# Expert outputs of a mixture layer: per-token gathers from DRAM in place of one-hot scatters on the matmul engine

## The reference

```python
logits = (xt @ router_w).astype(jnp.float32)
top_val, top_idx = lax.top_k(logits, TOP_K)            # TOP_K = 2
gates = jax.nn.softmax(top_val, axis=-1)
combine = jnp.einsum("nk,nke->ne", gates, jax.nn.one_hot(top_idx, N_EXPERTS, dtype=jnp.float32))
y = jnp.zeros((B * T, D), dtype=jnp.float32)
for e in range(N_EXPERTS):
    y = y + combine[:, e:e + 1] * swiglu(xt, w_gate[e], w_up[e], w_down[e]).astype(jnp.float32)
```

## Time and profile before

| what | value |
|---|---|
| median of 3 runs | 1693.59 us |
| lowest, highest | 1688.69, 1699.33 us |
| the profiled execution | 1676.64 us |
| its span | 1674.8 us |
| mean granted clock of PE over the span | 0.988 of full |
| instructions on PE | 25372 matmuls, as many weight loads |
| moved by DMA | 433.37 MB, 259 GB/s over the span |

### The profile page before, as it was taken

One profiled execution on the slowest core, in us unless ns is written; L12 is line 12 of the kernel. 1 busy time (PEld: TensorE's weight loads), 2 busy tenths in 40 slices (PEclk: granted clock), 3 DMA queues, 4 the chain that ended last, 5 costly groups with the idle time before them and its releaser, 6 DMA issues.

```text
span 1674.8 us, 53009 instructions
## 1 busy us (share of the span) xinstructions
PE 1549.9 (93%) x25372; PEld 1349.2 (81%) x25372; DVE 270.4 (16%) x481; ACT 184.6 (11%) x389; POOL 143.9 (9%) x164
## 2 busy tenths in 40 slices
PE   7999999999999998789898899999899898998996
PEld 6788577777686964788888898889888898898986
DVE  3443310000243433200010010010000000000102
ACT  3223220000222323100000000000000000000001
POOL 2233200000032422100000000000000000000000
PEclk9999999999999998799999999999999999999999
DMA  9213244444422235599999999999999999999970
GB/s 315 98 39 126 101 151 151 151 151 139 168 93 79 111 116 220 216 378 366 355 361 351 344 373 360 379 343 379 360 341 375 346 367 377 349 365 386 365 275 27
DMA packets 147652, 433.37 MB, mean 259 GB/s; under 512 B 9050, under 2 KB 33884, under 8 KB 147436
## 3 DMA queue, kind: packets, MB, share of 16 engines
q1 hardware_dynamic: 146556, 427.75, 69.5%
q0 software_dynamic: 672, 2.14, 0.4%
q10 hardware_dynamic: 208, 0.08, 0.0%
HBM read 428.89 MB, written 1.05 MB: 257 GB/s over the span
## 4 chain that ended last, share of the span: by engine, by line
PE 89%; issue 5%; DVE 3%; ACT 1%; POOL 1%; SPq 0%; DMA 0%; DVEq 0%
PE ps L964 34%; PE ps L984 17%; PE ps L852 9%; PE ps L581 8%; PE ps L863 4%; PE ps L730 3%; PE ps L592 3%; PE ps L1008 2%; PE ps L716 1%; PE ps L701 1%; PE ps L712 1%; PE ps L932 1%; PE ps L607 1%; PE ps L614 1%; PE ps L722 1%
## 5 line engine op out<-in xcount | busy, mean ns | idle before, releaser
L984 PE MATMUL ps<-LT_sb,ring 128*64 128x88 f32 x5376 | 216.7, 240 | 19.9 <-issue 18.7
L964 PE MATMUL ps<-wpost,ring 128*64 128x88 f32 x5376 | 217.2, 241 | 18.2 <-issue 17.2
L984 PEld LDWEIGHTS ps<-LT_sb,ring 128*64 128x64 f32 x5376 | 208.5, 137 | 28.9 <-issue 27.7
L964 PE MATMUL ps<-AT_sb,ring 128*64 128x88 f32 x5376 | 214.6, 240 | 16.9 <-issue 16.9
L964 PEld LDWEIGHTS ps<-wpost,ring 128*64 128x64 f32 x5376 | 209.8, 138 | 25.0 <-issue 24.4
L964 PEld LDWEIGHTS ps<-AT_sb,ring 128*64 128x64 f32 x5376 | 207.9, 137 | 23.1 <-issue 22.8
L852 PEld LDWEIGHTS ps<-hT_sb,ring 128*128 128x128 f32 x768 | 136.0, 190 | 24.6 <-issue 9.1
L852 PE MATMUL ps<-hT_sb,ring 128*128 128x256 f32 (+1 forms) x768 | 155.7, 362 | 0.0
L581 PE MATMUL ps<-hT_sb,ring 128*128 128x256 f32 x608 | 136.3, 382 | 0.0
L581 PEld LDWEIGHTS ps<-hT_sb,ring 128*128 128x128 f32 x608 | 115.2, 192 | 16.1 <-DVE late L1366 0.5
L1655 DVE TENSOR_TENSOR LT_sb<-BM,ps 128x704 f32<-128x704 f32 (+1 forms) x32 | 25.5, 797 | 547.3 <-PE ps L964 547.3
(11 more groups left out here) (269 smaller groups left out, 1173.5 us busy)
## 6 DMA issues: line engine op xcount, KB each, us to landing
ring<-in_moe_w_gate SPq DMA_DIRECT2D x84, 1024.0 KB, 6.7
ring<-in_moe_w_up SPq DMA_DIRECT2D x84, 1024.0 KB, 7.4
ring<-in_moe_w_down SPq DMA_DIRECT2D x84, 1024.0 KB, 7.3
late<-in_moe_w_up SPq DMA_DIRECT2D x28, 1024.0 KB, 6.8
late<-in_moe_w_gate SPq DMA_DIRECT2D x28, 1024.0 KB, 6.7
late<-in_moe_w_down SPq DMA_DIRECT2D x28, 1024.0 KB, 6.9
ring<-in_ffn_w_gate SPq DMA_DIRECT2D x11, 1024.0 KB, 5.5
ring<-in_ffn_w_up SPq DMA_DIRECT2D x11, 1024.0 KB, 8.1
```

Source lines behind the costliest of these rows:

```text
L964: ins = mm(o[lo:lo + P // 2, :], w[:, i, m * P + lo:m * P + lo + P // 2], xgT[e % 2][:, k, :], start=(k == 0 and m % 4 == 0), stop=(k == K ...
L984: ins = mm(o[lo:lo + P // 2, :], d[:, i, m * P + lo:m * P + lo + P // 2], moe_hid[:, 2 * j + i, :], start=(first and m % 4 == 0), stop=las ...
```

## The change

For experts 0 to 6, `y_tok` is no longer scattered by PE. ACT stores its 88 rows to a DRAM tensor `y_rows` of 616 rows and one row of zeros. DVE works out, in expert 6, for each token and each of its two experts, the row number in `y_rows` (from the rank and from the expert's number, by `w8` = 8 minus the number); where the expert is expert 7, or the rank lies outside this round's 88 slots, it is the zero row. In expert 7, POOL fetches by four indirect DMAs (two choices x two token tiles) the row of each token into `y_found`, 128 rows of 1024, and DVE adds it, times `g1` or `g2`, to `moe_y`. There is one `y_found`, so each fetch waits for the addition before it. Expert 7 is scattered on PE as before. `y_copy` waits for the store before (of the expert before). `sel1` and `sel2` are kept: their products with the gates now go to `lg2` and `cand`. The waits of `gather` and of `y_transposes` on scatters and on the one-hot copies are replaced or gone.

PE:

```diff
                 if e >= 2:
-                    pe.wait_ge(moe_acc[1], per_round(r, e - 1, N_EXP))
-                elif e == 1:
-                    pe.wait_ge(ohT_ready, per_round(r, 1, N_EXP))
+                    pe.wait_ge(y_act, per_round(r, e - 1, N_EXP))
+                    pe.wait_ge(y_dve, per_round(r, e - 1, N_EXP))
...
                     m_in(r, "g", e, 0)
                     if e:
                         m_down(r, e - 1, MOE_CH - 1)
-                    else:
-                        onehot_transposes(r, 0)
                     m_in(r, "u", e, 0)
                     if e:
                         y_transposes(r, e - 1)
                     m_in(r, "g", e, 1)
-                    if e:
-                        scatter(r, e - 1, 0)
                     m_down(r, e, 0)
-                    if e:
-                        scatter(r, e - 1, 1)
                     m_in(r, "u", e, 1)
...
                     m_down(r, e, 1)
-                    if e < N_EXP - 1:
-                        onehot_transposes(r, e + 1)
+                    if e == N_EXP - 2:
+                        onehot_transposes(r, N_EXP - 1)
...
                 y_transposes(r, N_EXP - 1)
+                scatter_last(r)
```

ACT, behind `y_copy` and ahead of `m_silu(e, 1)`:

```diff
+            def y_store(r, e):
+
+                act.wait_ge(y_act, per_round(r, e + 1, N_EXP))
+                act.wait_ge(y_dve, per_round(r, e + 1, N_EXP))
+                act.dma_start(y_rows[e * SLOTS:(e + 1) * SLOTS, :], y_tok).then_inc(y_stored, 16)
```

DVE (`rows_to_find` is 14 small instructions on 4 to 16 columns with waits between them; `add_last` is `accumulate` of expert 7, with a wait for the four additions):

```diff
+            def add_found(r, i):
+
+                j, t = divmod(i, TT)
+                dve.wait_ge(y_landed, per_round(r, 16 * (i + 1), 16 * 2 * TT))
+                if i == 0:
+                    dve.wait_ge(y_zero_row, 16)
+                V.scalar_tensor_tensor(moe_yv[:, t, :], y_found, (g1, g2)[j][:, t:t + 1], moe_yv[:, t, :],
+                                       ALU.mult, ALU.add).then_inc(y_added, 1)
...
                     m_hidden(r, e, 0)
                     if e:
                         y_copy(r, e - 1)
-                        accumulate(r, e - 1)
                     if e < N_EXP - 1:
                         choose(r, e + 1)
+                    if e == N_EXP - 2:
+                        rows_to_find(r)
                     m_hidden(r, e, 1)
                     if e < N_EXP - 1:
                         gathered(r, e + 1)
+                    else:
+                        add_found(r, 0)
+                        add_found(r, 1)
                     m_hidden(r, e, 2)
+                    if e == N_EXP - 1:
+                        add_found(r, 2)
+                        add_found(r, 3)
                     m_hidden(r, e, 3)
```

POOL, behind the clearing of `moe_y`:

```diff
+            pool.dma_start(y_rows[Y_ROWS:Y_ROWS + 1, :], moe_y[0:1, 0:D]).then_inc(y_zero_row, 16)
...
+            with pool.Fori(0, rounds) as r:
+                pool.wait_ge(y_at_step, per_round(r, 14, 14))
+                pool.wait_ge(y_stored, per_round(r, 16 * (N_EXP - 1), 16 * (N_EXP - 1)))
+                for i in range(2 * TT):
+                    if i:
+                        pool.wait_ge(y_added, per_round(r, i, 2 * TT))
+                    pool.sem_inc(y_asked, 1)
+                    pool.indirect_dma_start(y_found, None, y_rows, bass.IndirectOffsetOnAxis(ap=y_at[:, i:i + 1], axis=0))\
+                        .then_inc(y_landed, 16)
```

More of the change, by code:

```diff
@@ L99 @@
 assert ROUND_UNITS % N_UNIT == 0
+Y_ROWS = (N_EXP - 1) * SLOTS
 N_STEPS = 25
@@ L197, in build @@
         rounds_i = sb("rounds_i", 1, I32)
+        y_at = sb("y_at", 2 * TT, I32)
+        y_rows = nc.dram_tensor("y_rows", [Y_ROWS + 1, D], F32, kind="Internal").ap()
         def v3(t, a, lo=0, n=None):
@@ L281, in build @@
         ident_bf = sbe[:, 0:P // 2].bitcast(BF16)
-        onehotT = [X_sb[0:SLOTS, j * T:(j + 1) * T] for j in range(2)]
+        onehotT = X_sb[0:SLOTS, 0:T]
+        y_found = hT_sb[:, D:2 * D]
+        picked = [rn, nsum, ba, sss]
+        y_rank, y_left, y_valid, y_row = (c[:, 0:2 * TT] for c in (aa, sabs, sln, spl))
         moe_sg = v3(BM, 8, 0, 8 * SLOTS)
@@ L337, in build @@
         yT_act, yT_dve, yT_ps = (sem(n) for n in ("yT_act", "yT_dve", "yT_ps"))
+        y_stored, y_zero_row, y_at_step, y_asked, y_landed, y_added = (
+            sem(n) for n in ("y_stored", "y_zero_row", "y_at_step", "y_asked", "y_landed", "y_added"))
         moe_acc = [sem(f"moe_acc{t}") for t in range(TT)]
@@ L997, in y_transposes, with scatter_last @@
                 ins.then_inc(yT_ps, 1)
[L999 to L1010, removed]
+            def scatter_last(r):
+                e = N_EXP - 1
+                pe.wait_ge(ohT_ready, per_round(r, 1, 1))
+                pe.wait_ge(y_act, per_round(r, e + 1, N_EXP))
+                pe.wait_ge(y_dve, per_round(r, e + 1, N_EXP))
+                for t in range(TT):
+                    for half in range(2):
+                        ins = mm(bank(2 * t + half), onehotT[:, t * P:(t + 1) * P],
+                                 y_tok[:, half * 512:(half + 1) * 512], start=True, stop=True)
+                    ins.then_inc(scatter_ps, 1)
             pe.wait_ge(part_ready, 3 * TT)
@@ L1043, in _ @@
                 y_transposes(r, N_EXP - 1)
+                scatter_last(r)
                 for t in range(TT):
-                    scatter(r, N_EXP - 1, t)
-                for t in range(TT):
-                    pe.wait_ge(moe_acc[t], per_round(r, N_EXP, N_EXP))
+                    pe.wait_ge(moe_acc[t], per_round(r, 1, 1))
         @block.scalar
@@ L1255, in _, with onehotT_copy @@
             rounds = act.value_load(rounds_i[0:1, 0:1], min_val=1, max_val=3)
-            def onehotT_copy(r, e):
-                act.wait_ge(ohT_ps, per_round(r, e + 1, N_EXP))
-                A(onehotT[e % 2], bank(6)[0:SLOTS, 0:T], ACT.Copy).then_inc(ohT_ready, 1)
+            def onehotT_copy(r):
+                act.wait_ge(ohT_ps, per_round(r, 1, 1))
+                A(onehotT, bank(6)[0:SLOTS, 0:T], ACT.Copy).then_inc(ohT_ready, 1)
             def yT_copy(r, e):
@@ L1636, in y_copy, with rows_to_find, done @@
                 dve.wait_ge(yT_ps, per_round(r, e + 1, N_EXP))
+                if e:
+                    dve.wait_ge(y_stored, per_round(r, 16 * e, 16 * (N_EXP - 1)))
                 V.tensor_copy(y_tok[:, 512:D], bank(7)[0:SLOTS, :]).then_inc(y_dve, 1)
[L1639 to L1642, removed]
+            def rows_to_find(r):
+                def done(n):
+                    dve.wait_ge(y_at_step, per_round(r, n, 14))
+                for i, (chosen, by) in enumerate(((sel1, tv(rank)), (sel2, tv(rank)), (sel1, bcm(w8, TT)), (sel2, bcm(w8, TT)))):
+                    V.tensor_tensor(tv(picked[i]), tv(chosen), by, ALU.mult).then_inc(y_at_step, 1)
+                done(4)
+                for i in range(4):
+                    to = (y_rank, y_left)[i // 2]
+                    V.tensor_reduce(to[:, i % 2 * TT:(i % 2 + 1) * TT], tv(picked[i]), AX_X, ALU.add)\
+                        .then_inc(y_at_step, 1)
+                done(8)
+                V.tensor_scalar(y_valid, y_rank, 0.0, None, ALU.is_ge).then_inc(y_at_step, 1)
+                V.scalar_tensor_tensor(y_row, y_left, -float(SLOTS), y_rank, ALU.mult, ALU.add).then_inc(y_at_step, 1)
+                done(9)
+                V.scalar_tensor_tensor(y_valid, y_rank, SLOTS - 0.5, y_valid, ALU.is_le, ALU.mult).then_inc(y_at_step, 1)
+                done(11)
+                V.scalar_tensor_tensor(y_valid, y_left, 1.5, y_valid, ALU.is_ge, ALU.mult).then_inc(y_at_step, 1)
+                done(12)
+                V.scalar_tensor_tensor(y_row, y_row, float(N_EXP * SLOTS - Y_ROWS), y_valid, ALU.add, ALU.mult)\
+                    .then_inc(y_at_step, 1)
+                done(13)
+                V.tensor_scalar(y_at[:, :], y_row, float(Y_ROWS), None, ALU.add).then_inc(y_at_step, 1)
@@ L1675, in _ @@
                 y_copy(r, N_EXP - 1)
-                accumulate(r, N_EXP - 1)
+                add_last(r)
                 V.tensor_scalar(rank, rank, -float(SLOTS), None, ALU.add).then_inc(route_step, 1)
```

36 lines of the change are left out of this document (21 added, 15 removed).

## The result

The changed kernel takes 1700.84 us (median of 20 runs, 1681.33 to 1707.73), the kernel before 1688.66 us on the same chips (20 runs). The ratio is 1.0063, 95% interval 1.0042 to 1.0085: slower by 10.6 us (7.1 to 14.4). That is within 1%, the case given 0.73, and inside the stated range, but on the other side of no change than the -3 us that were forecast. The ratio is formed without the run of 1707.73 us, over 1.5% above the fastest, and not from the two medians, which are 12.2 us apart. The first median of before, 1693.59 us of 3 runs, lay 5 us over that of 20 runs. The profiled execution of the changed kernel took 1688.47 us, its span is 1686.6, against 1676.64 and 1674.8 before.

The account below looks back on a forecast made before the run. The prediction took PE's instruction fetch, late behind the weight traffic, to bound the kernel. -7 (PE) + 3 (stores) + 1 (gathers) = -3 us gave 1690.6 us, with 1669 to 1704 for 8 times in 10.

Parts of the forecast that it names:

- the case given 0.73: Whole kernel: instruction fetching keeps the pace, 1690.6 us, own range 1682 to 1699, within 1% of before; chance 0.73.
- What bounds the kernel: Expert layer: PE's instruction blocks of 256 arrive late behind weight traffic, 0.7 us lost per 5.07 us; weights never late.
- Scatters off PE: Experts 0 to 6: removing 14 scatters and 7 transpose pairs saves 1.0 us per expert, 7 us in all.
- the two estimates: PE saving per expert: none from comparing 42-unit stretches, 0.5 us from some 25 fewer instructions, a tenth of a block.
- The stretch of expert 0: First 42 units, without scatters: 3.85 us less PE work, yet 122.70 us against 122.56 for the six with two scatters.
- The ceiling of 28.4 us: Most that PE's part could give: 26.7 us for 14 scatters and about 1.7 us for 7 transpose pairs.
- Stores: Seven stores of 0.36 MB on ACT's queue lie in the way of instruction fetches: 3 us added, bounds 0 to 6.9.
- Gathers: Expert 7: four fetches of 8 us round trip, hidden behind products; two compete with instruction fetches, 1 us added.
- The second (PE's work in full): Expert layer: PE's saved work comes off in full, 1665.2 us, or half, about 1679; chance 0.16.
- The third (gather round trip): Expert 7: a round trip from 16 us stalls DVE's products and PE; 1719 us at 25, 1736 at 30; chance 0.07.
- The fourth (a constant delay of every fetch): Two further queues delay all 161 instruction blocks by 0.15 us each, 24 us, 1715 us in all; chance 0.04.
- The profile's signs: Expected trace: PE busy some 28 us less, issue gaps up some 20 us, landing some 7 us, 42 units some 121 us.

Follow-up runs that it names:

- the single run: Kernel before, all scatters kept, with the seven stores of 0.36 MB added on ACT's queue: ratio 1.0014 to the kernel before.
- the fourfold ones: Each store issued four times, in the kernel before with scatters kept (1.0082) and in the changed kernel without gathers and additions (1.0098).
- the difference on one chip: Whole change (1.0058) against the change without stores, its gathers fetching one zero row (1.0033), both as ratios to the kernel before: 0.25%.
- the first difference without gathers: Changed kernel without gathers and additions (1.0057) against the change without stores, gathers and additions (0.9999), both as ratios to the kernel before.
- one pair of runs: Changed kernel (1.0063) and the same without gathers and additions (1.0057), ratios to the kernel before, on two chips: 0.06%.
- the other: Change without stores, gathers fetching one zero row (1.0033), and change without stores, gathers and additions (1.0003), ratios to the kernel before: 0.30%.

## Why the prediction was wrong

*What bounds the kernel.* Right, and shown three ways: the gaps at every 256 instructions end 1.3 to 1.6 us behind an instruction transfer, they vanish when the weight stream is halved, and idle PE falls from 13.4 and 12.4 us to 6.9 and 4.4 in two stretches where only fewer transfers are queued. The Trainium skill's rule in "Runtime: NRT & Kernel Launch", section "Instruction fetch mechanics", that fetching is hidden behind execution, held with half the traffic (no gap in 109.73 us) and not with the whole.

*Scatters off PE: the step that failed.* "I take 1.0, near the two estimates: 7 us in all." Measured: 0.9999 and 1.0003, no saving, within some 5 us; the gaps took it back, 5.2 us per expert where the scatters had been. The stretch of expert 0 had said so (122.70 against 122.56 us). The two estimates were 0 and 0.5 us; 1.0 lies above both, and was what one stretch can't exclude, taken as if it were a finding. The second estimate, 0.5 us per expert for the instructions that are gone, is too small to be seen in these intervals. The ceiling of 28.4 us was slightly low too: seven transpose pairs are the 14 matmuls of the earlier trace rows, 2.4 us and not 1.7.

*Stores: the size is not far off, within the noise.* Forecast 3 us; 2.4 by the single run, 3.5 and 4.1 by the fourfold ones, 4.2 by the difference on one chip, and 9.8 by the first difference without gathers (0.58%). That they cost by lying in the way of fetches fits the cost that vanishes with half the traffic, and is not shown apart from it.

*Gathers: hidden as forecast, traffic under-priced.* The round trip was taken as 8 us; DVE waited 10.0 under traffic and 5.3 behind it. No product waited. Their price in traffic was forecast at 1 us, with 2.8 as its bound for two gathers. Three fell into the traffic, as the prediction's own times have it (the third asked for at 1610.7, traffic until 1623); three are 4.3 us by the same sum. It is 1 us by one pair of runs and 5 by the other; which is not settled.

*The sum.* -7 + 3 + 1 = -3 us was forecast; 0 + 4 and 1 to 5 make +5 to +9, and the whole was measured as +10.6 and +9.8. Of the 13 us or so between forecast and result, 7 are the PE term; the rest is stores and gathers, put at 4 and measured at 9 to 10 together. Had the PE term been taken from the natural experiment as it stood, the forecast would have been +4, on the right side. Direction hung on that one term, since the PE part was the only one with a minus. That the result lies inside the stated range says little for the sum: the bounds 0 to 14 saved and 0 to 9.7 added make 1679.6 to 1703.3 us, not the 1682 to 1699 given in the first case.

*Rivals.* The second (PE's work in full) was false on this kernel and true with half the traffic, where the change is worth 31 us. The third (gather round trip) did not happen: the last addition was 10.4 us early. The fourth (a constant delay of every fetch) would have been +24 us; it did not happen, and four times the stores cost 13.8 and 16.5 us. A block lasts 745.57 us x 128 / 16468 = 5.8 us on the average of the six stretches, under the 5.9 named for this case.

*The profile's signs.* Forecast were gaps up by some 20 us; they went up by 36 (70.6 to 106.8), part of which is the quick execution of before: with its stores added, the kernel before has 87.5 us of them in a trace of 1697.8 us. PE's busy time fell by 25.0 where 28 were expected. Units land as early as before. 42 units take 124.3 us, where 121 were forecast.

## What to carry to other kernels

Before taking work off an engine that is 93% busy, ask what its gaps wait for: where its instructions come late, the time follows the fetches, and work is free as far as there are gaps close behind it to fill (here one scatter, not two). A stretch that already runs without the work in question is worth more than any price list; take its number as it stands. In this kernel, with the DMA engines 97% held, replacing on-chip work by DRAM traffic was the wrong trade, though no product ever waited for a transfer.

## What the runs showed of the hardware that was not expected

Late instructions can tie PE to the DMA engines' rate although each weight unit lands some 39 us before its use: with 1 MB units the 42-unit stretch took about 122.6 us with 353 to 369 GB/s moved, with 0.5 MB units 109.73 us at 204 GB/s and no gap.

Limiting the transfers in flight to two shortened the first two stretches to 115.8 and 116.3 us, but cost stream rate (341 and 337 GB/s there). PE's waits for instructions fell from 70.6 to 13.3 us, and 64.9 us of waits for weights came in their place. Used only where the lead may be consumed, the limit gave 0.38%.

PE work is not symmetric around the working point: some 28 us less gave 0 us (within some 5), 26.7 us more cost 17.9 us (13 to 23). The gaps outside the scatters' neighbourhood did not take up any of it.
